# Lag matrices on four column tiles, U loads behind two weight units, sample probabilities ahead of a z tile, stops between convolution taps

## What is computed

```python
u_a, z_a, u_b, z_b, q, z_x, g_a, g_b, g_x = jnp.split(h @ p['w_in'], IN_SPLITS, axis=-1)
y_a, s_new = s5_branch(u_a, s0, ...)          # 32 groups x 16 channels, 64 complex states, scan over positions
v_b = u_b[..., :E_CONV] * jax.nn.sigmoid(u_b[..., E_CONV:])
c_b, buf_new = causal_depthwise_conv(v_b, conv_buf, p['conv_w'], p['conv_b'])   # 31 taps
o_x = attention of q over 256 memory tokens (own keys for the prompt, cached ones for each sample)
m = sigmoid(g_a) * o_a + sigmoid(g_b) * o_b + sigmoid(g_x) * o_x
x = x + m @ p['w_out']
```

## Time and profile before

| | |
|---|---|
| median of three runs | 1157.01 us |
| the profiled execution, its own time | 1154.06 us |
| its span, first to last instruction | 1152.3 us |
| mean granted TensorE clock | 0.980 |

### The profile page before, as it was taken

The page is one execution under the profiler, slowest core; times in us unless marked ns, Lnnn a source line. Parts: engine busy times, 40 slices in busy tenths (PEclk is TensorE's granted clock), DMA queues, the critical chain, the costliest instruction groups (busy, mean ns, idle before and its releaser), DMA issues.

```text
span 1152.3 us, 20452 instructions
## 1 busy us (share of the span) xinstructions
PE 1086.5 (94%) x8274; PEld 1015.4 (88%) x8274; DVE 813.7 (71%) x1209; ACT 419.4 (36%) x714; POOL 460.0 (40%) x329
## 2 busy tenths in 40 slices
PE   3999999989999999999989799998999999999995
PEld 3658998969999999999956799896999999999994
DVE  4868888998966784444489888989996867644412
ACT  4612553324453342222433245322444445222222
POOL 2037544454433224444313845445443322444440
PEclk8899999989999999999999899999999999999997
DMA  7235516784416723445432453478432564334422
GB/s 218 80 122 153 205 56 202 193 177 115 130 56 139 200 98 120 129 129 164 138 109 75 112 202 101 137 230 180 131 115 79 115 150 153 120 122 135 131 84 74
DMA packets 225300, 155.01 MB, mean 135 GB/s; under 512 B 48690, under 2 KB 201706, under 8 KB 223142
## 3 DMA queue, kind: packets, MB, share of 16 engines
q1 hardware_dynamic: 220454, 144.14, 44.8%
q10 hardware_dynamic: 4752, 9.57, 2.3%
HBM read 130.38 MB, written 24.24 MB: 134 GB/s over the span
## 4 chain that ended last, share of the span: by engine, by line
PE 66%; DVE 16%; DMA 5%; SPq 2%; POOL 2%; ACT 2%; issue 1%; DVEq 0%; ACTq 0%
PE acc L723 41%; PE mp L1059 12%; DVE cacc L1459 6%; PE mp L764 3%; PE acc L1040 2%; POOL w_lo L615 2%; DMA w_st<-in_w_in 2%; PE mp L664 2%; PE mp L935 1%; PE mp L826 1%; PE mp L864 1%; DMA y_scratch<-U 1%; DVE V L1453 1%; SPq L510 1%; DVE X L1453 1%
## 5 line engine op out<-in xcount | busy, mean ns | idle before, releaser
L615 POOL TENSOR_TENSOR w_lo<-w_st,w_hi 128x512 fp32r<-128x512 f32 x288 | 439.8, 1532 | 592.7 <-ACT w_hi L1145 592.1
L1145 ACT CAST w_hi<-w_st 128x512 fp32r<-128x512 f32 x288 | 177.4, 620 | 564.3 <-PE acc L723 370.4
L723 PE MATMUL acc<-h_hi,w_hi 128*128 128x260 f32 x1600 | 329.4, 287 | 10.0 <-POOL w_lo L615 9.0
L723 PE MATMUL acc<-h_lo,w_hi 128*128 128x260 f32 x1600 | 322.5, 283 | 0.0
L723 PE MATMUL acc<-h_hi,w_lo 128*128 128x260 f32 x1600 | 321.9, 283 | 0.0
L723 PEld LDWEIGHTS acc<-h_hi,w_hi 128*128 128x128 f32 x1600 | 247.6, 189 | 20.4 <-issue 18.1
L723 PEld LDWEIGHTS acc<-h_hi,w_lo 128*128 128x128 f32 x1600 | 247.0, 189 | 0.0
L723 PEld LDWEIGHTS acc<-h_lo,w_hi 128*128 128x128 f32 x1600 | 246.8, 189 | 0.0
L1459 DVE SCALAR_TENSOR_TENSOR cacc<-vx,cw,cacc 128x512 f32<-128x512 f32 x232 | 192.8, 902 | 1.5
L1059 PE MATMUL mp<-br_hi,w_hi 128*128 128x260 f32 x384 | 77.4, 283 | 4.7 <-POOL w_lo L615 4.7
L1059 PE MATMUL mp<-br_lo,w_hi 128*128 128x260 f32 x384 | 77.3, 283 | 0.0
(11 more groups left out here) (300 smaller groups left out, 1447.6 us busy)
## 6 DMA issues: line engine op xcount, KB each, us to landing
w_st<-in_w_in SPq DMA_DIRECT2D x208, 256.0 KB, 3.3
g_scratch<-xT ACTq DMA_DIRECT2D x32, 260.0 KB, 2.7
xT<-g_scratch SPq DMA_DIRECT2D x8, 1040.0 KB, 7.0
kb<-in_cache_mem_k SPq DMA_DIRECT2D x16, 512.0 KB, 5.3
kb<-in_cache_mem_v SPq DMA_DIRECT2D x16, 512.0 KB, 4.9
w_st<-in_w_out SPq DMA_DIRECT2D x32, 256.0 KB, 2.8
x_scratch<-xT SPq DMA_DIRECT2D x2, 2080.0 KB, 7.5
xT<-x_scratch SPq DMA_DIRECT2D x4, 1040.0 KB, 6.1
```

The source lines that it names most:

```text
L615: pool.tensor_tensor(w_lo[:, slot, :], w_st[:, slot, :], w_hi[:, slot, :].bitcast(F32), ALU.subtract).then_inc(w_staged_free, 1)
L723: last = pe.matmul(acc_ps[pair][:, a, 0:HC], w[:, slot, kk * P:(kk + 1) * P], x[:, k, a, :], start=(k == 0 and p == 0), stop=(k == KT - 1 ...
L1145: act.copy(w_hi[:, c % SLOTS, :], w_st[:, c % SLOTS, :]).then_inc(w_hi_done, 1)
```

## The change

- The lag matrices of four pairs r go to four column tiles of the array (32 columns each), so that the output lies on 128 partitions and in one bank; `kt`, `dt`, the identity (`eye`, now made by one reduce) and the skip column `dcol` follow this layout, and so does the store of `kt`.
- SP loads x1.1 and e3.0 before the loads of `U`.
- ACT copies `psT` before it evacuates x0.1.
- DVE waits in the taps of tiles 0, 2 and 3 for named low words (`low_made`): 4 stops in tile 0, 2 in tile 2, 7 in tile 3.
- The sample outputs are taken (`ox_done`) behind tap 22 of tile 3, not behind its last tap.

```diff
 # sync
                 half("x1", 0)
+                half("x1", 1)
+                half("e3", 0)
                 wait(sp, l, "u_out", 16)
                 wait(sp, l, "U_clear", 1)
...
-                half("x1", 1)
-                half("e3", 0)
                 for b in range(4, NB):
                     wait(sp, l, "pvs_done", b - 3)
                     cache_load(cache_mem_v, b)
...
-                    sp.dma_start(kh.rearrange("(q e) h x -> (e h) q x", e=2), kt[:, :, :]).then_inc(sm["k_out"], 16)
+                    sp.dma_start(kh.rearrange("(r y) h x -> (y h) r x", r=2), kt[:, :, :]).then_inc(sm["k_out"], 16)
 # tensor, lag_matrices(f)
-                    for r in range(QH):
+                    for g in range(2):
                         for ri in range(2):
-                            last = pe.matmul(mp[0:2 * H, r // 4, (r % 4) * P:(r % 4 + 1) * P],
-                                             bd[:, ri, f * QH + r, :, :].rearrange("p e h -> p (e h)"),
-                                             V[:, ri, r, 0:T, :].rearrange("p t h -> p (t h)"),
-                                             start=(ri == 0), stop=(ri == 1))
+                            for j in range(4):
+                                r = 4 * g + j
+                                last = pe.matmul(mp[32 * j:32 * j + 32, 0, g * P:(g + 1) * P],
+                                                 bd[:, ri, f * QH + r, :, :].rearrange("p e h -> p (e h)"),
+                                                 V[:, ri, r, 0:T, :].rearrange("p t h -> p (t h)"),
+                                                 start=(ri == 0), stop=(ri == 1), tile_position=(0, 32 * j))
 # scalar
                 one("x0", 0, to_z(2))
-                one("x0", 1, to_z(2))
+                ready(1, use["x0"], unit["x0"] + 1)
                 wait(act, l, "psT_tr", 1)
                 wait(act, l, "psT_clear", 1)
                 act.copy(psT[:, :, :, 0:16], ...).then_inc(sm["psT_ev"], 1)
+                to_z(2)(0, 1)
 # vector
-            tt(eye2[:, :], ident[0:2 * H, 0:H], ident[0:2 * H, H:2 * H], ALU.add)
+            run(dve.tensor_reduce(eye[:, :], ident[:, :].rearrange("p (b h) -> p h b", h=H), op=ALU.add, axis=AX.X))
...
-                convolution(0, 0, TAPS)
+                def low_made(name, k, h):
+
+                    dve.wait_ge(w_staged_free, 2 * (l * UNITS + unit[name] + k) + h + SLOTS + 1)
+
+                convolution(0, 0, 13)
+                for first, half in ((13, 0), (17, 1), (21, 2), (25, 3)):
+                    low_made("q0", half // 2, half % 2)
+                    convolution(0, first, first + 4 if half < 3 else TAPS)
...
-                    run(dve.tensor_copy(kt[:, :, :].rearrange("h q x -> h (q x)"), mp[0:2 * H, 0:2, :].rearrange("h b x -> h (b x)")))
+                    run(dve.tensor_copy(kt[:, :, :].rearrange("h q x -> h (q x)"), mp[:, 0, 0:2 * P]))
...
-                convolution(2, 22, TAPS)
-                convolution(3, 0, 10)
+                low_made("x1", 0, 0)
+                convolution(2, 22, 27)
+                low_made("x1", 0, 1)
+                convolution(2, 27, TAPS)
+                low_made("x1", 1, 0)
+                convolution(3, 0, 5)
+                low_made("x1", 1, 1)
+                convolution(3, 5, 10)
                 keep_lags(0)
-                convolution(3, 10, TAPS)
+                for first, name, half in ((10, "e3", 0), (14, "e3", 1), (18, "e3", 2)):
+                    low_made(name, half // 2, half % 2)
+                    convolution(3, first, first + 4)
                 wait(dve, l, "oxT_tr", 1)
                 for hd in range(HEADS):
                     run(dve.tensor_copy(q[:, hd, :, 4 * C:HC], ...))
                 dve.sem_inc(sm["ox_done"], 1)
+                for first, name, half in ((22, "e3", 3), (26, "e4", 0)):
+                    low_made(name, half // 2, half % 2)
+                    convolution(3, first, first + 4 if first < 26 else TAPS)
```

More of the change, by code:

```diff
@@ L99, in build @@
         ones = sb("ones", [P, P])
-        eye2 = sb("eye2", [2 * H, H])
+        eye = sb("eye", [P, H])
         vec = sb("vec", [P, 80])
         cw = sb("cw", [P, TAPS * ET])
-        dcol = sb("dcol", [2 * H, Q])
+        dcol = sb("dcol", [P, 4])
         pw = sb("pw", [P, 2, Q, T + 1])
@@ L154, in build @@
         srow = ur("srow", 768, [P, 2, P])
-        drow = ur("drow", 1024, [Q, 2 * H])
+        drow = ur("drow", 1024, [4, P])
         dtrow = ur("dtrow", 1040, [80, 2])
@@ L199, in build @@
         s2 = rr("s2", 1152, [P, QH * (T + 1) * H])
-        dt = rr("dt", 13072, [2 * H, QH * H])
+        dt = rr("dt", 13072, [P, 2 * H])
         t1 = rr("t1", 10256, [P, QH * (T + 1) * H])
@@ L215, in build @@
         wkv = at(wd_at, 0, 24 * P, "wkv", [P, 2, 2 * E])
-        kt = at(wd_at, 0, 24 * P, "kt", [2 * H, QH, T * H])
+        kt = at(wd_at, 0, 24 * P, "kt", [P, 2, T * H])
         cacc = at(wd_at, 16 * P, 24 * P, "cacc", [P, 2, T, C])
@@ L330, in param_loads @@
                 sp.dma_start(cwrow[:, :], conv_w[l].rearrange("k (i c) -> (k i) c", c=P)).then_inc(sm["p_in"], 16)
-                sp.dma_start(drow[:, :], ssm_d[l].rearrange("(q x) -> q x", x=2 * H)).then_inc(sm["p_in"], 16)
+                sp.dma_start(drow[:, :], ssm_d[l].rearrange("(q x) -> q x", x=P)).then_inc(sm["p_in"], 16)
             def state_loads(l):
@@ L672, in param_turns @@
                 transpose(mp[:, 2, P:P + TAPS * ET], cwrow[:, :], TAPS * ET)
-                last = transpose(mp[0:2 * H, 2, 256:256 + Q], drow[:, :], Q)
+                last = transpose(mp[:, 2, 256:260], drow[:, :], 4)
                 last.then_inc(sm["par_tr"], 1)
@@ L1482, in columns @@
                 run(dve.tensor_copy(cw[:, :], mp[:, 2, P:P + TAPS * ET]))
-                dve.tensor_copy(dcol[:, :], mp[0:2 * H, 2, 256:256 + Q]).then_inc(sm["par_ev"], 1)
+                dve.tensor_copy(dcol[:, :], mp[:, 2, 256:260]).then_inc(sm["par_ev"], 1)
                 wait(dve, l, "par_ev", 1)
@@ L1732, in keep_lags @@
                         wait(dve, l, "k_out", 16)
-                    run(dve.tensor_copy(kt[:, :, :].rearrange("h q x -> h (q x)"), mp[0:2 * H, 0:2, :].rearrange("h b x -> h (b x)")))
+                    run(dve.tensor_copy(kt[:, :, :].rearrange("h q x -> h (q x)"), mp[:, 0, 0:2 * P]))
                     dve.sem_inc(sm["k_free"], 1)
                     ta = dt[:, :].rearrange("h (q x) -> h q x", x=H)
-                    tt(ta, eye2[:, :].unsqueeze(1).to_broadcast([2 * H, QH, H]),
-                       dcol[:, f * QH:(f + 1) * QH].unsqueeze(2).to_broadcast([2 * H, QH, H]), ALU.mult)
+                    tt(ta, eye[:, :].unsqueeze(1).to_broadcast([P, 2, H]),
+                       dcol[:, 2 * f:2 * f + 2].unsqueeze(2).to_broadcast([P, 2, H]), ALU.mult)
                     tt(kt[:, :, 0:H], kt[:, :, 0:H], ta, ALU.add)
```

## The result

The changed kernel took 1160.72 us against 1158.18 for the kernel before, both medians of 20 runs: a ratio of 1.0024, interval 1.0014 to 1.0034. By the ratio it is slower by 2.8 us; the forecast was 10.6 us faster, and the measured time lies above its range. The profiled execution of the changed kernel took 1158.5 (span 1156.7, mean granted clock 0.971 against 0.980).

What follows compares the result with a forecast made beforehand. PE, busy 94% of the span, was taken as the bound, with DVE arriving together with it at x_done. Layer 0 gains 3.1 us and layer 1 7.5, so 1157.01 - 10.6 = 1146.4 us; range 1136 to 1156.

Steps and rivals of the forecast that it cites:

- The half clock at `x_done`: At L965, PE arrives early, waits about 5 us for x_done, then half clock: 1.7 us lost per layer.
- The stops of tile 0: PE's low-word waits at q0 (2.9 and 6.1 us) go; 1.5 us stay in layer 0, 5.9 in layer 1.
- the two waits of about 1 us at q1.0: PE would wait for q1.0's low word instead: 1.2 us in layer 1, 0.8 in layer 0.
- Up to 2.5 us later: Tile 1 would start up to 2.5 us later on DVE because of the stops in tile 0.
- 0.6, by choice: Allowance of 0.6 us for first scores and probabilities, which stand behind DVE's later tile 1.
- SP and ACT: New load and copy order: psT's 5.08 us wait and its half clock go; cache loads cost PE 1 to 2 us.
- they move: The 10.5 us of PE's waits for psT bring nothing by themselves; they move to L965.
- rival 2: The stops make DVE the bound: nine stops in tiles 2 and 3 cost 13.5 us a layer, 1173 us; chance 0.12.
- the rivals: Four: DVE not the bound (1132 us, 0.17); stops bind DVE (0.12); taps don't hold low words (0.11); tiling brings nothing (1150).
- Lag matrices: Four column tiles: 3.68 us falls to 1.9 (ends 0.92 and 3.84), gaining 1.8 us a layer pass.
- DVE to `x_done`: DVE's gains less the stops' costs sum to -1.1 us; x_done at 311.4, L965 at 311.5 in place of 313.00.
- Rival 3: Taps don't hold low words, held one tap at most; 7.4 us not gained, 1153.8 us, up to 1157; chance 0.11.

Runs made afterwards that it cites:

- fill_e7: The changed kernel with one block of 48 projection products (e7) taken ahead of PE's wait for x_done(0), not behind the products that follow it; 0.9948 of the time before.
- no_stop0: The changed kernel without the stops in tile 0, its 31 taps in one run again; 1.0025 of the time before.
- fill_late_stops: fill_no_lag with the stops of tile 0 behind taps 17, 21, 24 and 27 in place of 13, 17, 21 and 25; 0.9903 of the time before.
- fill_no_lag: fill_e7 with the lag matrices as before the change (32 products one after another, copied from two banks); 0.9928 of the time before.

## Why the prediction was wrong

**The half clock at `x_done`, mis-sized.** "A wait of 5.08 was followed by half clock, and 1.7 us were lost; I charge this again." The wait itself was forecast (about 5 us; 1.05 and 4.00 came). But the rows behind the 1.7 are of thick products. Here the wait stands between thin ones: PE is busy at half clock for 10.30 and 11.10 us, half of it lost, 10.7 us in place of 3.4, on the path. PE's rows say the same. Against the kernel before, L967 starts 1.4 us early in layer 0 and 2.3 in layer 1; the products behind e7 (L664 at 325.55 and 878.59, before 322.19 and 875.62) start 3.4 and 3.0 us late: 4.8 + 5.2 = 10.0 us lost between. `fill_e7` shows that this place decides the sign: with the wait filled the change is 0.5% faster.

**The stops of tile 0, +7.4 forecast, 1.5 measured alone and nothing in the change.** The 9.0 us of waits for `w_lo` went as forecast, and the two waits of about 1 us at q1.0 did not come. The cost to DVE was wrong in two steps. "Up to 2.5 us later" for tile 1 was 5.4: the first stop idles 3.86 us, because it stands behind tap 13, which ends at 77.78 + 2.73 = 80.5, and the low word begins only at 82.83 in the kernel before, behind ACT's cast (POOL there):

```profile
82.83 14.81 POOL L615 TENSOR_TENSOR w_lo<-w_st,w_hi 128x512 fp32r<-128x512 f32 x4 [11.76 <-ACT w_hi L1145]
```

And once one operation of POOL has got in, all take turns with the taps, `glu_v` and the low words of q1 too, not four low words only. The "0.6, by choice" for scores and probabilities was 3.18 and 4.3 us with half clock behind. The run of taps of layer 1, put at 645.3, was over at 644.2: 645.3 is the end of the low word. `no_stop0` shows that the two sides cancel. `fill_late_stops` shows the idle time gone with a later stop; its gain over `fill_no_lag`, 0.25%, has overlapping intervals.

**SP and ACT: right in kind.** `psT`'s waits went; the cache loads went out at 242.40 (239 forecast) and cost 4.54 and 3.9 us of PE's gain (1 to 2 forecast), where DVE covers them. The gain that went to L965, "they move", is what the waits show. That the orders need the stops of tiles 2 and 3 was not seen. It is the reverse of rival 2: of these stops one in each layer idles DVE, for 1.35 us, and together they bring 10.7 us. So the kernel became slower by none of the rivals.

**Lag matrices.** 1.08 us, near the lower end of 0.92 to 3.84, where 1.9 was taken. In the change the part gives 2.5 us, not clear of noise, against 3.6 forecast, alone and with e7 ahead nothing that can be told: at fold 0 PE waits for it elsewhere, as forecast.

**DVE to `x_done`: the number came out, by luck.** L967 starts at 311.40, for 311.5. But the 1.1 us of the sum should have been won ahead of DVE's first input matrix (`wt`), and it starts there at 271.36, where it started at 271.40. In layer 1 it is 825.23 against 824.83. In layer 0 DVE had come to the sample probabilities 1.9 us late from tile 0 (228.23 against 226.32), which the sum has at nothing; from there to `wt` it won 1.95. The 1.4 us by which DVE's last step before `x_done` ends earlier (311.09 against 312.48) were won behind `wt`, where the sum has no term, 1.0 of them in the same two copies just ahead of it (DVE before, then changed):

```profile
310.32 1.96 DVE L1809 COPY X<-X 64x576 f32<-64x576 f32 x2
...
271.36 1.23 DVE L1456 TENSOR_TENSOR wt<-pw,bb 128x1024 f32<-128x1024 f32 x1
...
309.95 0.94 DVE L1830 COPY X<-X 64x576 f32<-64x576 f32 x2
```

Why they got shorter was not tested.

**Rival 3 and its rule.** The Trainium skill (SBUF — State Buffer, Who interferes with whom) would have a low word held for one instruction at most. Behind a break the trace agrees (1.51 to 1.79 us, in the middle of a run); ahead of the first break it does not (10.608).

The terms do not add up exactly: 10.0 - 3.4 = 6.6 too little charged at L967, 7.4 for tile 0 and 1.1 for the lag part make 15.1 us, and 13.4 are missing. The 1.7 us between are within the intervals of the parts.

## What to carry to other kernels

A wait that moves is charged at its new place with that place's clock: look at what TensorE runs just before and after it. If these are thin products, try a block of thick products in the wait; here it gained 8.8 us. Moves on a queue and the events that free its slots are one edit; try them together. If one engine's long run of instructions starves another, one break at the right place may do (4.5 us here), and a stop ahead of the moment when its event can come only idles. When a forecast time comes out, check the terms that made it too.

## What the runs showed that was not expected

- A wait of 1.05 us was enough for 6.8 to 10.3 us at half clock between thin products, and 64 thin products behind a wait kept the half clock for 17 us. Why waits of the same length were followed by 6.8 us in some kernels and 10.3 in others stays open.
- One break of a run of taps, with no event to wait for, lets POOL in for the rest of the run. Why an unbroken run shuts it out in tiles 0 and 2 while it gets in in tile 1 stays open.
